# Chunk states of a Mamba-2 layer kept with channels on the partitions

## What is computed

```python
chunk_states = jnp.einsum("bcsgn,bcsge,bcsgep->bcgepn", Bc, decay_to_end, xd).reshape(b, nc, H, P, N)
chunk_decay = jnp.exp(a_cum[:, :, -1, :])
def step(h, inp):
    s, d = inp
    return h * d[:, :, None, None] + s, h
h_final, h_prev = lax.scan(step, h0, (chunk_states, chunk_decay))
y_off = jnp.einsum("bclgn,bcgepn,bclge->bclgep", Cc, h_prev, jnp.exp(a_cum))
y = (y_diag + y_off).reshape(b, L, H, P)
```

## Time and profile before

| | |
|---|---|
| median of three runs | 1005.31 us (1002.44 to 1006.59) |
| profiled execution | 1002.74 us; span from first to last instruction 1001.0 us |
| mean granted TensorE clock | 0.948 of full speed |
| busy share of the span | TensorE 91%, VectorE 66%, ScalarE 48%, GpSimd 16% |
| the four groups | 52.4 to some 411 us |

### The profile page before, as it was taken

One profiled execution on the slowest core, in us unless ns is written; L12 is line 12 of the kernel. 1 busy time (PEld: TensorE's weight loads), 2 busy tenths in 40 slices (PEclk: granted clock), 3 DMA queues, 4 the chain that ended last, 5 costly groups with the idle time before them and its releaser, 6 DMA issues.

```text
span 1001.0 us, 20427 instructions
## 1 busy us (share of the span) xinstructions
PE 911.0 (91%) x7371; PEld 891.3 (89%) x7371; DVE 661.3 (66%) x1040; ACT 482.3 (48%) x897; POOL 161.5 (16%) x101
## 2 busy tenths in 40 slices
PE   6889699978878896599999999999999999989996
PEld 5689698968878896499999999999999999989996
DVE  4679998997899899975464645445555444554533
ACT  5467647655765576653444433233233233333344
POOL 6302451352137124500000000000000000000000
PEclk7989798979998897699999999999999999999999
DMA  7136546443654354313231433232223332222222
GB/s 196 46 93 185 140 122 170 129 134 111 183 158 134 95 181 140 100 49 101 86 103 43 127 90 99 85 103 84 84 84 93 98 102 84 84 84 85 84 61 85
DMA packets 158835, 108.02 MB, mean 108 GB/s; under 512 B 5024, under 2 KB 146876, under 8 KB 158204
## 3 DMA queue, kind: packets, MB, share of 16 engines
q1 hardware_dynamic: 119780, 76.15, 25.9%
q10 hardware_dynamic: 38592, 30.54, 10.2%
q0 software_dynamic: 400, 0.55, 0.3%
HBM read 95.35 MB, written 12.14 MB: 107 GB/s over the span
## 4 chain that ended last, share of the span: by engine, by line
PE 60%; DVE 20%; issue 7%; ACT 5%; DVEq 1%; ACTq 0%; POOL 0%; POOLq 0%
PE bank L1256 39%; PE bank L1415 18%; DVE acc L897 5%; DVE wlo L791 4%; DVE zh L972 3%; DVE st L961 1%; DVE hs L928 1%; DVE xd L911 1%; ACT em L571 1%; ACT thx L548 1%; PE bank L1317 1%; DVE dtx L955 1%; DVE yr L965 1%; PE bank L1326 1%; DVE yob L945 1%
## 5 line engine op out<-in xcount | busy, mean ns | idle before, releaser
L1256 PE MATMUL bank<-hhi,whi 128*128 128x260 f32 x1664 | 342.9, 288 | 10.9 <-ACT ext L538 10.0
L1256 PE MATMUL bank<-hhi,wlo 128*128 128x260 f32 x1664 | 339.1, 286 | 0.0
L1256 PE MATMUL bank<-hlo,whi 128*128 128x260 f32 x1664 | 339.0, 286 | 0.0
L1256 PEld LDWEIGHTS bank<-hhi,whi 128*128 128x128 f32 x1664 | 261.0, 192 | 14.9 <-ACT ext L538 11.6
L461 ACT ACTIVATE whi<-raw 128x1024 fp32r<-128x1024 f32 x136 | 143.8, 1057 | 253.8 <-PE bank L1256 154.1
L1256 PEld LDWEIGHTS bank<-hlo,whi 128*128 128x128 f32 x1664 | 260.8, 192 | 0.0
L1256 PEld LDWEIGHTS bank<-hhi,wlo 128*128 128x128 f32 x1664 | 260.7, 191 | 0.0
L791 DVE TENSOR_TENSOR wlo<-raw,whi 128x1024 fp32r<-128x1024 f32 x132 | 169.9, 1287 | 41.1 <-ACT whi L461 39.2
L1415 PE MATMUL bank<-hhi,whi 128*128 128x260 f32 x512 | 104.6, 286 | 4.1 <-DVE hlo L1074 4.1
L1415 PE MATMUL bank<-hlo,whi 128*128 128x260 f32 x512 | 103.9, 285 | 0.0
L1415 PE MATMUL bank<-hhi,wlo 128*128 128x260 f32 x512 | 103.6, 284 | 0.0
(11 more groups left out here) (213 smaller groups left out, 984.5 us busy)
## 6 DMA issues: line engine op xcount, KB each, us to landing
raw<-in_sc_w_in SPq DMA_DIRECT2D x64, 512.0 KB, 4.0
raw<-in_ssd_w_in SPq DMA_DIRECT2D x40, 512.0 KB, 3.9
abc<-a_rows ACTq DMA_DIRECT2D x16, 512.0 KB, 4.6
st<-in_state_ssm ACTq DMA_DIRECT2D x16, 512.0 KB, 4.8
out_new_ssm_s<-st ACTq DMA_DIRECT2D x16, 512.0 KB, 3.7
raw<-in_ssd_w_out SPq DMA_DIRECT2D x16, 512.0 KB, 3.8
raw<-in_sc_w_out SPq DMA_DIRECT2D x16, 512.0 KB, 3.8
bcbc<-bc_rows ACTq DMA_DIRECT2D x4, 1024.0 KB, 7.7
```

The lines of the kernel that those rows point to most:

```text
L1256: mm = pe.matmul(b[:, 0:TH], w[:, slot, k * P:(k + 1) * P], h[:, k, cols], start=(k == 0 and i == 0), stop=(k == KT - 1 and i == 2))
```

## The change

The chunk states are held turned: channels on the partitions, state index along the free axis, in hsT, which lies in yob's memory. For that the operands of within's state products are swapped. The decay of a channel is then one number for each partition (cdch, gathered once from cdbc ahead of the loop), and the recurrence is a copy and three operations of 128x128, of which the last writes the final state to finb directly. The products of across need the other layout: a new step lift(q) on TensorE turns the first three states into bank 7, a new step evac_states(q) on ScalarE copies them to hs, and across waits for that copy. The copy of the final state in add_earlier and the transpose in across go. recur(q) waits for the store of finb, for lift(q - 1) and for the end of add_earlier(q - 1). TensorE's and ScalarE's orders change as the diff shows.

```diff
@@ -96,7 +96,7 @@
         abc = sb("abc", [P, 2, SEQ])
         em = sb("em", [P, 2, SEQ])
         ech = sb("ech", [P, SEQ])
-        hs = sb("hs", [P, NC, P])
+        hs = sb("hs", [P, NC - 1, P])
         yob = sb("yob", [P, SEQ - Q])
         finb = sb("finb", [P, NS])
         st = sb("st", [P, 2, NB * NS])
@@ -125,12 +125,14 @@
         dtcol = sb("dtcol", [P, NC, HEADS])
         dte = sb("dte", [P, NC, HEADS])
         cdbc = sb("cdbc", [P, NC, HEADS])
+        cdch = sb("cdch", [P, NC, TILES])
         dtch = sb("dtch", [P, TILES, NB])
         dcch = sb("dcch", [P, TILES, NB])
         ssq = sb("ssq", [P, 8])
         eps = sb("eps", [P, 1])
 
 
+        hsT = yob[:, :].rearrange("p (c n) -> p c n", n=NS)
         flat = ybuf[:, :, :].rearrange("p a b -> p (a b)")
         x_nat = [flat[:, t * D:(t + 1) * D] for t in range(4)] + [flat[0:NB, 4 * D:5 * D]]
         cs_nat = flat[0:NB * PRE0, 5 * D:5 * D + XBC]
@@ -211,7 +213,8 @@
         seg_done = sem("seg_done")
         abc_in, e_done, ech_done, m_done = sem("abc_in"), sem("e_done"), sem("ech_done"), sem("m_done")
         s_done, sd_done, rec, o_done = sem("s_done"), sem("sd_done"), sem("rec"), sem("o_done")
-        fin_done, fin_st = sem("fin_done"), sem("fin_st")
+        fin_st = sem("fin_st")
+        hs_t, hs_done = sem("hs_t"), sem("hs_done")
         yd_done, yo_done, y_done = sem("yd_done"), sem("yo_done"), sem("y_done")
         st_ld, st_st = [sem(f"st_ld{s}") for s in range(2)], [sem(f"st_st{s}") for s in range(2)]
         dtx_done, t1_done, dh_done, st_new, t2_done = (sem(n) for n in ("dtx_done", "t1_done", "dh_done", "st_new", "t2_done"))
@@ -581,8 +584,12 @@
                         act.activation(ech[0:HD, Q:SEQ], abc[0:HD, 0, Q:SEQ], ACT.Exp)
                         act.activation(ech[HD:P, Q:SEQ], abc[HD:P, 1, Q:SEQ], ACT.Exp).then_inc(ech_done, 1)
 
+                    def evac_states(q):
+                        act.wait_ge(hs_t, g * 4 + (q + 1))
+                        act.activation(hs[:, :, :].rearrange("p c n -> p (c n)"), bank[7][:, 0:(NC - 1) * P], ACT.Copy).then_inc(hs_done, 1)
+
                     def final_state(q):
-                        act.wait_ge(fin_done, g * 4 + (q + 2))
+                        act.wait_ge(rec, g * 16 + 4 * (q + 1))
                         act.dma_start(fin_out[ds(g * 512 + q * P, P), :], finb[:, :]).then_inc(fin_st, 16)
 
                     def load_state(q):
@@ -636,6 +643,7 @@
                     decay(1)
                     tanh_conv(4)
                     evac_conv(5, g * 4 + 3)
+                    evac_states(0)
                     decay_channels(1)
                     final_state(0)
                     load_abc(2)
@@ -646,6 +654,7 @@
                     decay(2)
                     scale_state(1)
                     evac_z(6, 0)
+                    evac_states(1)
                     final_state(1)
                     decay_channels(2)
                     load_abc(3)
@@ -656,15 +665,17 @@
                     decay(3)
                     squares(0)
                     scale_state(2)
-                    decay_channels(3)
                     load_state(3)
                     squares(1)
+                    evac_z(8, 2)
+                    evac_states(2)
+                    decay_channels(3)
                     final_state(2)
-                    evac_z(8, 2)
                     scale_state(3)
-                    final_state(3)
                     store_state(2)
                     evac_z(9, 3)
+                    evac_states(3)
+                    final_state(3)
                     store_state(3)
                     squares(2)
 
@@ -777,7 +788,6 @@
             dve.sem_inc(yo_done, 1)
             dve.sem_inc(gate_done, 2)
             dve.sem_inc(yr_done, 1)
-            dve.sem_inc(fin_done, 1)
             dve.sem_inc(yd_done, 1)
             dve.sem_inc(sz_done, 1)
             dve.sem_inc(out_evac, 4)
@@ -873,8 +883,11 @@
                 dve.tensor_copy(dtch[rows, :, :], by[:, :, 0:NB]).then_inc(dt_v, 1)
                 dve.tensor_copy(dcch[rows, :, :], by[:, :, NB:2 * NB]).then_inc(dt_v, 1)
                 dve.tensor_copy(dch[rows, :], dbc[rows, :].rearrange("p (j h) -> p j h", h=2)[:, :, half]).then_inc(dt_v, 1)
-            dve.wait_ge(dt_v, 23)
             dve.wait_ge(dt_s, 10)
+            for half, lo in ((0, 0), (1, HD)):
+                rows = slice(lo, lo + HD)
+                dve.tensor_copy(cdch[rows, :, :], cdbc[rows, :, :].rearrange("p c (j h) -> p c j h", h=2)[:, :, :, half]).then_inc(dt_v, 1)
+            dve.wait_ge(dt_v, 25)
             dve.wait_ge(lo_done, 2 * SLOT)
 
             with dve.Fori(0, GROUPS // 2) as G:
@@ -921,14 +934,16 @@
 
                     def recur(q):
                         dve.wait_ge(s_done, g * 4 + (q + 1))
-                        dve.tensor_copy(hs[:, 0, :], bank[5][:, 0:P]).then_inc(rec, 1)
+                        dve.wait_ge(hs_t, g * 4 + q)
+                        dve.wait_ge(y_done, g * 4 + q)
+                        dve.tensor_copy(hsT[:, 0, :], bank[5][:, 0:NS]).then_inc(rec, 1)
                         for c in range(1, NC):
-                            dve.wait_ge(rec, g * 28 + (7 * q + 2 * c - 1))
-                            for h in range(2):
-                                dve.scalar_tensor_tensor(hs[:, c, h * HD:(h + 1) * HD], hs[:, c - 1, h * HD:(h + 1) * HD],
-                                                         cdbc[:, c, ds(g * 8 + (2 * q + h), 1)],
-                                                         bank[5][:, c * P + h * HD:c * P + (h + 1) * HD],
-                                                         ALU.mult, ALU.add).then_inc(rec, 1)
+                            dve.wait_ge(rec, g * 16 + (4 * q + c))
+                            if c == NC - 1:
+                                dve.wait_ge(fin_st, g * 64 + 16 * (q + 1))
+                            dve.scalar_tensor_tensor(hsT[:, c, :] if c < NC - 1 else finb[:, :], hsT[:, c - 1, :],
+                                                     cdch[:, c, ds(g * 4 + q, 1)], bank[5][:, c * NS:(c + 1) * NS],
+                                                     ALU.mult, ALU.add).then_inc(rec, 1)
 
                     def skip(q):
                         dve.wait_ge(sd_done, g * 4 + (q + 2))
@@ -940,8 +955,6 @@
                     def add_earlier(q):
                         dve.wait_ge(o_done, g * 4 + (q + 1))
                         dve.wait_ge(ech_done, g * 4 + (q + 2))
-                        dve.wait_ge(fin_st, g * 64 + 16 * (q + 1))
-                        dve.tensor_copy(finb[:, :], bank[7][:, 0:NS]).then_inc(fin_done, 1)
                         dve.tensor_tensor(yob[:, :], bank[7][:, Q:SEQ], ech[:, Q:SEQ], ALU.mult).then_inc(yo_done, 1)
                         dve.wait_ge(yo_done, g * 4 + (q + 2))
                         dve.wait_ge(yd_done, g * 8 + (2 * q + 3))
@@ -1290,7 +1303,7 @@
                             mm = transpose(bank[4][:, c * Q:(c + 1) * Q], BT[:, c * Q:(c + 1) * Q])
                         mm.then_inc(tb_done, 1)
                         if gg == 1:
-                            pe.wait_ge(rec, g * 28)
+                            pe.wait_ge(rec, g * 16)
                         for c in range(NC):
                             mm = pe.matmul(bank[5][:, c * Q:(c + 1) * Q], BT[:, c * Q:(c + 1) * Q], CT[:, c * Q:(c + 1) * Q],
                                            start=True, stop=True)
@@ -1312,9 +1325,9 @@
                         if q == 0:
                             pe.wait_ge(cbm_done, g + 1)
                         else:
-                            pe.wait_ge(rec, g * 28 + 7 * q)
+                            pe.wait_ge(rec, g * 16 + 4 * q)
                         for c in range(NC):
-                            mm = pe.matmul(bank[5][:, c * P:(c + 1) * P], Bs[:, c, :], xdd[:, c, :], start=True, stop=True)
+                            mm = pe.matmul(bank[5][:, c * NS:(c + 1) * NS], xdd[:, c, :], Bs[:, c, :], start=True, stop=True)
                         mm.then_inc(s_done, 1)
                         pe.wait_ge(m_done, g * 4 + (q + 1))
                         if q == 0:
@@ -1327,11 +1340,15 @@
                                                em[:, h, c * Q:(c + 1) * Q], start=True, stop=True)
                         mm.then_inc(sd_done, 1)
 
+                    def lift(q):
+                        pe.wait_ge(rec, g * 16 + 4 * q + 3)
+                        pe.wait_ge(yo_done, g * 4 + (q + 1))
+                        for c in range(NC - 1):
+                            mm = transpose(bank[7][:, c * P:(c + 1) * P], hsT[:, c, :])
+                        mm.then_inc(hs_t, 1)
+
                     def across(q):
-                        pe.wait_ge(rec, g * 28 + 7 * (q + 1))
-                        pe.wait_ge(yo_done, g * 4 + (q + 1))
-                        pe.wait_ge(fin_done, g * 4 + (q + 1))
-                        transpose(bank[7][:, 0:NS], hs[:, NC - 1, :])
```

(11 more changed lines are left out.)

## The result

The changed kernel takes 1032.84 us as the median of four executions (1029.56 to 1033.0), beside 1005.17 for the kernel before: 1.0271 of its time, 95% interval 1.0252 to 1.0291. The profiled execution took 1032.76 us, its span is 1030.9 us, 29.9 more than before.

The account below looks back on a forecast made before the run. VectorE was taken to set the pace of the groups. Waits less savings gave +8.1 us a group, +32.4 for four, +0.4 ahead: 1035.5 from the profiled 1002.7, 1038 on the median; 1037 taken, range 1020 to 1047.

Parts of the forecast that it names:

- The mechanism: VectorE, which sets the groups' pace, idles because across waits for ScalarE's copy, queued behind other work: +8.1 us a group.
- Waits for across: VectorE's idle time ahead of yob in each group: 2.2, 0.2, 4.6 and 2.8 us for q = 0 to 3.
- q = 1: Second step of a group: copy behind evac_z(6), across at the lower clock, 0.2 us wait; 1.5 us for the store.
- q = 2: Third step of a group: copy behind squares(1), which waits for gate(1), and evac_z(8); VectorE waits 4.6 us (3.6 to 5.3).
- The store: The recurrence's last step waits for the previous final state to land, 3.7 us after issue: 1.5 us at q = 1, 0.4 at q = 3.
- q = 0: First step of a group: copy behind evac_conv(5), whose first tap waits for silu(4); VectorE idles 2.2 us (1.8 to 3.0).
- VectorE's savings: Per recurrence 0.37 us, plus 0.20 for the final state's copy in add_earlier: 2.3 us a group, 9.1 for the kernel.
- rival A: Kernel gets faster: the four waits sum to less than VectorE's 2.3 us saving; up to 9 us gained, 996 us; chance 0.05.
- What comes back: Addition behind yob gets shorter at q = 0 and q = 2, GpSimd being through by then: -0.7 and -0.6 us.
- Ahead of the loop: Two small copies for cdch, run once before the groups: about 0.4 us added.
- TensorE's added work at nothing: Two more transposes for each q, under 0.83 us, lie where TensorE idles: no cost, at most 9 us uncovered.
- Rival C: TensorE becomes a bound too: across(3) ends some 11 us later, delaying the next group's projections; 1049 us; chance 0.10.

Follow-up runs that it names:

- e1: Changed kernel, but at q = 2 ScalarE copies the states right behind decay(3) and TensorE does across(2) ahead of within(3): 1016.46 us.
- e2: Changed kernel, but at q = 3 ScalarE copies the states and stores the final one ahead of evac_z(9): 1020.05 us.
- e10: Kernel before with ScalarE's order around evac_z(8) as changed, and TensorE's across(2) behind within(3) and a wait for that tanh: 1018.49 us.
- e3: Changed kernel, but at q = 0 ScalarE copies the states ahead of evac_conv(5) and TensorE does across(0) ahead of turn(2): 1029.92 us.
- e6: e4 with a 128x128 copy into an unused buffer put back into add_earlier, where the final state was copied before: 1000.71 us.
- e4: Changed kernel with the state copies early at every q, and final_state(0) and final_state(2) issued ahead of the wait for yob: 1001.15 us.

## Why the prediction was right

It said 1037 (1020 to 1047) and slower at 0.93; 1032.84 came. The mechanism was the forecast one; the size came lower, 27.7 us between the medians where the sum had 32.8. A group's period rose by 6.8 us on average (27.0 in all), where 8.1 (32.4) were forecast. By its steps, for the third group where nothing else is said:

- **Waits for across**: 9.5 us measured against 9.8. By q 2.22, 0.28, 4.19 and 2.85 against 2.2, 0.2, 4.6 and 2.8. In the second and fourth groups the wait at q = 1 was 0.95 and the one at q = 2 was 4.9: at q = 2 TensorE's three products took 1.65 us there, at a granted clock of 0.50, and 0.94 in the third group, at 1.00. Over all four groups the waits are 40.8 us against 39.2. e1, e2 and e10 show that these waits are what the time goes into. The terms written out for q = 2 add up to 4.75 us and not to 4.6.
- **q = 1 was met by luck**: VectorE reached yob 1.1 us sooner than forecast, as the store held it up less, and the products were ready 1.0 us sooner. Half of that is TensorE's granted clock, 1.00 there (304 to 305), where the forecast had taken the price at 0.50: 0.94 us and not 1.49. The two errors cancel.
- **The store**: the term that was mis-sized, 0.6 us at q = 1 (none in the second group) and none at q = 3, against 1.5 and 0.4. I took the 3.7 us from issue to landing that this store had the earlier trace rows; in the changed kernel it had 2.4 in the same place:

```profile
out_new_ssm_p<-finb ACTq DMA_DIRECT2D x1, 64.0 KB, 2.4
```

  The fit that the Trainium skill states (DMA: Bandwidth & Descriptors, Anatomy of one DMA), by my estimate from it 2.15 us for this size, lies nearer to that than my row; it is for another issuing engine, and by it alone there would have been no wait. Why the same transfer landed sooner was not tried by itself, but the traces point at one thing, the load of weights (512 KB) that SyncE issues just ahead of it, before and after:

```profile
272.32 0.37 SPq L256 DMA_DIRECT2D raw<-in_ssd_w_in  x1
...
287.06 0.37 SPq L259 DMA_DIRECT2D raw<-in_ssd_w_in  x1
```

  Before, the store is issued 0.48 us behind that load (at 272.80), and in all four groups 0.5 us behind it; it takes 3.7 us each time. In the changed kernel VectorE's own wait at q = 0 moves it to 2.7 us behind the load (at 289.72), and it takes 1.6 to 2.5. In e3, which takes that wait away, it is 0.7 to 1.1 us behind and takes 3.3 to 4.7. So the forecast wait at q = 0 seems to have shortened the next one. A fixed duration for a transfer was the weak step, not the mechanism: with e3's order the wait was 1.20 us.
- **VectorE's savings**: 0.29 us a recurrence against 0.37. The operation of 128x128 lasts 0.35 us, as the slope gave (0.344); the longer idle time ahead of the last was not in my sum. Of the copy's 0.2 us little would have come, by e6, had the waits not freed the addition from GpSimd. The prediction took both in full; it was rival A's price of 996 that hung on that, and e4 at 1001.15 shows how far off that price was.
- **What comes back**: the addition at q = 0 and q = 2 took 0.56 us each against 1.36 and 1.28 before, so 1.5 us, as against 1.3. In the second and fourth groups the one at q = 1 also fell, from 1.36 to 0.6. Over all four groups 8.2 us came back, where 5.2 were forecast.
- **Ahead of the loop**: 0.4 us for the two copies of cdch. They last 0.41 us together and VectorE waits for ScalarE's first tap behind them, 1.91 us instead of 2.36, so they cost nothing. That the groups start 1.7 us later comes from further ahead, from instructions that the change doesn't touch: VectorE's first product behind TensorE there (dte) starts at 51.40 instead of 49.74.
- **TensorE's added work at nothing**: three transposes last 0.49 us and lie ahead of waits; e4 shows the group shorter than before with all of them in it. Rival C, TensorE as a bound, did not come: across(3) did end some 10 us later in the group, but the fourth group takes 25.93 us from its first tap to its first recurrence before and after alike.

Over all four groups the measured terms close: 40.8 for across, 1.9 for the store, less 7.8 for VectorE's savings and 8.2 for the additions, is 26.7 of the 27.0 us. The forecast was 39.2 + 7.6 - 9.1 - 5.2. It missed by the store above all, then by the additions, and the two smaller errors ran the other way. On the profiled execution the scatter outside the groups, 2.9 us in the same direction, hides half of the miss (1032.76 against 1035.5); that part was luck.

## What to carry to other kernels

When a step is handed to another engine in a kernel with hand-written orders, its cost is not its duration but what stands ahead of it in that engine's order: follow the chain from the engine that sets the pace, through each queue, back to it, and put the new step at the first place at which its input is there. The same change cost 28 us in one order and gained about 4 in another (e4). Undo such waits together, since one alone may hand its gain to the next, and read a saved instruction's worth from what the engine waits for right behind it.

## What the runs showed of the hardware

An addition on VectorE with two inputs in SBUF (128x384) lasts 0.56 us alone and stretches so as to end 0.41 us behind an operation of GpSimd that is already running: 290.66 against 290.25 before, 289.64 against 289.23 in e4, 290.07 against 289.66 in e6. At q = 0 and q = 2 before it is the same (274.19 against 273.78, 307.96 against 307.54). It is not slowed in proportion; it ends when the other is through. The Trainium skill (GPSIMD Engine Reference, Specifications) has the two engines share SBUF interfaces, with contention for VectorE's instructions with two SBUF inputs; the three traces agree. That a freed 0.2 us just ahead is lost whole by this, since GpSimd's own start lies ahead of what was freed, I had not expected.

The same store of 64 KB from ScalarE's queue landed in 1.6 us at the quickest and in 4.7 at the slowest (e3). At q = 0 it was slow where it was issued within 1.1 us behind a load of 512 KB (3.3 to 4.7 us in eight stores of the kernel before and e3) and quicker where it was issued 2.7 us behind it (1.6 to 2.5 in four of the changed kernel). No run moved the load alone.
